# One head group of the first attention reordered: query copies behind the maxima, one product in another bank, transposes behind a product, one weight split behind a scaling

## The reference, cut to what matters

```python
qkv = h @ w_in
q = rmsnorm_2(q.reshape(B, S, 16, 64), q_gain); k = rmsnorm_2(k...); 
scores = einsum(q, kb) * scale + bias            # each block of 128 rows sees itself and the block before
m = maximum(max(scores), sink); p = exp(scores - m)
probs = p / (sum(p) + exp(sink - m))
o = einsum(probs, vb);  return o @ w_out
```

## Time and profile before

| | |
|---|---|
| median of 3 runs | 2672.14 us (2670.05 to 2672.7) |
| the profiled execution | 2672.14 us, its span 2670.8 us |
| TensorE busy | 2642.5 us of the span |
| mean granted TensorE clock | 0.997 of full |
| the first attention | from about 1205 us to about 1360 us of the span |

### The profile page before, as it was taken

The page is one execution under the profiler, slowest core; times in us unless marked ns, Lnnn a source line. Parts: engine busy times, 40 slices in busy tenths (PEclk is TensorE's granted clock), DMA queues, the critical chain, the costliest instruction groups (busy, mean ns, idle before and its releaser), DMA issues.

```text
span 2670.8 us, 31302 instructions
## 1 busy us (share of the span) xinstructions
PE 2642.5 (99%) x12784; PEld 2216.1 (83%) x12784; DVE 1435.9 (54%) x2254; ACT 982.7 (37%) x1622; POOL 319.5 (12%) x388
## 2 busy tenths in 40 slices
PE   9999999999999999999999999999999999999999
PEld 8898888888887788779988888888888888888887
DVE  7637447565767444356874343453434676543433
ACT  4343334342454222236642222422223586422221
POOL 0000010000021000015530000100000586200000
PEclk9999999999999999999999999999999999999999
DMA  5322225523223444464323322233232101232321
GB/s 161 125 82 82 98 89 167 176 79 110 77 97 95 107 103 95 99 109 108 108 95 108 97 96 87 87 110 95 95 97 86 56 17 48 90 100 95 103 94 56
DMA packets 280936, 258.94 MB, mean 97 GB/s; under 512 B 40261, under 2 KB 275800, under 8 KB 280792
## 3 DMA queue, kind: packets, MB, share of 16 engines
q1 hardware_dynamic: 280775, 256.93, 32.4%
q10 hardware_dynamic: 16, 0.00, 0.0%
HBM read 242.23 MB, written 14.68 MB: 96 GB/s over the span
## 4 chain that ended last, share of the span: by engine, by line
PE 91%; DVE 4%; ACT 3%; issue 2%; POOL 1%; POOLq 0%; DVEq 0%; ACTq 0%
PE bank L1163 29%; PE bank L1165 29%; PE bank L1164 29%; PE bank L1321 1%; DVE Wl L1886 1%; POOL Wl L2446 0%; PE bank L1374 0%; PE bank L1174 0%; ACT Wh L1522 0%; PE bank L1470 0%; DVE Pl L2401 0%; POOL TMP L2453 0%; DVE Z L2393 0%; PE bank L1262 0%; DVE Hl L2358 0%
## 5 line engine op out<-in xcount | busy, mean ns | idle before, releaser
L1163 PE MATMUL bank<-Hh,Wl 128*128 128x512 f32 x2136 | 838.3, 392 | 1.8 <-DVE Hl L1905 1.8
L1165 PE MATMUL bank<-Hh,Wh 128*128 128x512 f32 x2136 | 832.1, 390 | 0.0
L1164 PE MATMUL bank<-Hl,Wh 128*128 128x512 f32 x2136 | 831.9, 389 | 0.0
L1886 DVE TENSOR_TENSOR Wl<-RAW,Wh 128x1024 fp32r<-128x1024 f32 (+2 forms) x420 | 493.7, 1219 | 161.9 <-ACT Wh L1522 161.1
L1522 ACT ACTIVATE Wh<-RAW 128x1024 fp32r<-128x1024 f32 (+2 forms) x454 | 441.1, 1022 | 363.1 <-PE bank L1165 337.3
L1163 PEld LDWEIGHTS bank<-Hh,Wl 128*128 128x128 f32 x2136 | 401.4, 188 | 88.1 <-DVE Hl L1905 3.1
L1163 PE MATMUL bank<-Ph,Wl 128*128 128x512 f32 x1200 | 470.9, 392 | 0.8 <-DVE Wl L1886 0.4
L1165 PEld LDWEIGHTS bank<-Hh,Wh 128*128 128x128 f32 x2136 | 401.4, 188 | 84.1
L1164 PEld LDWEIGHTS bank<-Hl,Wh 128*128 128x128 f32 x2136 | 401.6, 188 | 83.9 <-issue 1.7
L1165 PE MATMUL bank<-Ph,Wh 128*128 128x512 f32 x1200 | 467.3, 389 | 0.0
L1164 PE MATMUL bank<-Pl,Wh 128*128 128x512 f32 x1200 | 466.8, 389 | 0.0
(11 more groups left out here) (336 smaller groups left out, 2424.7 us busy)
## 6 DMA issues: line engine op xcount, KB each, us to landing
RAW<-in_ffn_wg SPq DMA_DIRECT2D x44, 1024.0 KB, 5.4
RAW<-in_ffn_wu SPq DMA_DIRECT2D x44, 1024.0 KB, 5.3
RAW<-in_ffn_wd SPq DMA_DIRECT2D x32, 1024.0 KB, 5.1
RAW<-in_w_up SPq DMA_DIRECT2D x22, 1024.0 KB, 5.1
RAW<-in_w_in SPq DMA_DIRECT2D x20, 1024.0 KB, 5.1
RAW<-in_ffn_wd SPq DMA_DIRECT2D x16, 768.0 KB, 4.4
bias_scratch<-M SPq DMA_DIRECT2D x16, 512.0 KB, 8.1
RAW<-in_w_down SPq DMA_DIRECT2D x8, 1024.0 KB, 5.2
```

Of the source, the lines that this page charges most:

```text
L1163: mm(o, ll, rh, start=start, stop=False)
L1164: mm(o, lh, rl, start=False, stop=False)
L1165: return mm(o, lh, rh, start=False, stop=stop)
L1886: tt(Wl[:, n % 3, x:y], RAW[:, n % 2, x:y], f(Wh[:, n % 3, x:y]), ALU.subtract).then_inc(*w_lo.up(*([("w_lo", n)] if i else [])))
```

## The change

In the first attention's loop four things move:

1. `q_out` of one unit per head now stands behind `a_scores(i)` and `a_soft(i)` instead of ahead of them. Unit 6 comes at i = 0, where it had come at i = 1.
2. `q_product(8)` (i = 1) takes its bank from `banks` instead of the single slot of `products`.
3. `q_turn(g)` at i = 2 and i = 6 comes behind `q_product(7 + i)` instead of ahead of it. At i = 10 there is no product to stand behind.
4. Tile 110 (the last group's query weights) is split, and tile 112 loaded, behind `a_exp(1)` and `a_norm(1)` instead of at the head of `q_product(8)`.

```diff
     def q_product(u, ring=None):
         g, b = u // 4, u % 4
         if b == 0:
-            tile[g] = next_tile("aq", g, 1)
+            tile[g] = next_tile("aq", g, 0 if g == 2 else 1)
         (ring or (products[0] if products else banks)).take(("aq", g, b))
...
     for i in range(16 + LV):
-        for u in {0: (5,), 1: (6, 7)}.get(i, (6 + i,) if i < 10 else ()):
-            q_out(u)
+        if i == 0:
+            q_out(5)
         if i == 10:
             banks.join(products[0])
         if i < 16:
             for m in range(2):
                 scored.take(("a_s", i, m))
             do("a_scores", i)
             do("a_soft", i)
+            if i < 10:
+                q_out(6 + i)
             if i == 1:
                 do("a_k_low", 1)
             if i + 2 < 16:
                 do("a_bias", i + 2)
         if 0 <= i - LT < 16:
             turns(i - LT)
         if i in (1, 5, 9):
             do("a_q_norm", i // 4 + 1)
+        if i < 9:
+            q_product(7 + i, banks if i == 1 else None)
         if i % 4 == 2 and i < 11:
             q_turn(i // 4 + 1)
-        if i < 9:
-            q_product(7 + i)
         if i >= LV:
             values(i - LV)
         if i < 16:
             do("a_exp", i)
             do("a_norm", i)
+        if i == 1:
+            split()
+            load()
```

More of the change, by code:

```diff
@@ L653, in order @@
     now["low"] = "pool"
-    attend_a_order(steps, banks, tmps, next_tile, norm_step, hkeys, pv, xv, h_new, h_pair, stats, add_x, do, dense)
+    attend_a_order(steps, banks, tmps, next_tile, split, load, norm_step, hkeys, pv, xv, h_new, h_pair, stats, add_x, do, dense)
     now["low"] = "dve"
@@ L697, in out_partial, with attend_a_order @@
     return run
-def attend_a_order(steps, banks, tmps, next_tile, norm_step, hkeys, pv, xv, h_new, h_pair, stats, add_x, do, dense):
+def attend_a_order(steps, banks, tmps, next_tile, split, load, norm_step, hkeys, pv, xv, h_new, h_pair, stats, add_x, do, dense):
     do("a_begin")
```

## The result

The changed kernel takes 2685.08 us (median of 4 runs, 2684.63 to 2686.61) against 2671.52 us of the kernel before beside it (4 runs): a ratio of 1.0052, 95% interval 1.004 to 1.0065. It is slower by 13.6 us. The forecast was 2684.7 us. The profiled execution took 2684.63 us, its span 2683.4 against 2670.8 us. TensorE's busy time hardly moved (2644.2 against 2642.5 us).

What follows compares the result with a forecast made beforehand. TensorE, busy for all but about 1%, was taken as the bound, so only its waits or clock count. 2672.1 + 8.2 (orders: 3.8 + 2.9 + 1.5) + 4.4 (clock) = 2684.7 us; range 2674 to 2691.

Steps and rivals of the forecast that it cites:

- The bound: Whole kernel: TensorE is busy for all but about 1%, so only its waits or a slower clock move the time.
- The three long ones: TensorE's idle ahead of products 8, 10 and 14: 3.9, about 4.1 and about 3.2 us.
- Parts 1 and 2: Product 8 waits for `a_k_low(1)` to vacate its bank, product 10 for ScalarE's chain behind the later `q_turn(1)`: 3.8 us together.
- Part 3: Tile 110's split behind `a_norm(1)`: removes head 1's 1.7 us wait, a gain already inside the 3.8 us; costs nothing.
- Part 4: `q_turn(2)` behind `q_product(13)`: transposes start one product later, ScalarE's chain is the same, so product 14 starts 2.9 us later.
- one sign: First attention: no more TensorE wait for L2500, the line of the head 1 scaling wait.
- Part 5: i = 9 and 10: unit 15's later sum and the shifted `banks` rotation start output unit 7 1.5 us later.
- `("a_qt", 3, 0)` now gets the slot of output unit 4: i = 10: the slot, no longer slot 5, is vacated by an addition, so `q_turn(3)` starts at 1302.3 instead of 1301.46.
- The clock: Behind the three long waits: two falls to half the granted clock at 2.2 us each, 4.4 us.
- Rival (a): The orders cost 8.2 us and the clock keeps its full level: 2680.3 us; chance 0.17.
- The orders' 8.2 us: First attention: cost of the new order without the clock, 3.8 + 2.9 + 1.5 = 8.2 us.

Runs made afterwards that it cites:

- run 6: The changed kernel with 28 unread transposes of the identity ahead of product 8 and 28 ahead of product 10: 2680.09 us, ratio 1.0032 to the kernel before.
- Run 3: The changed kernel with the low parts of the second head's keys made at i = 0 instead of i = 1: 2680.70 us, ratio 1.0031 to the kernel before.
- run 1: The changed kernel with the group's transposes ahead of the product again (i = 2 and 6): 2675.69 us, ratio 1.0015 to the kernel before.
- run 4: The changed kernel with the copies of units 9 and 13 ahead of the exponentials of heads 2 and 6 on ScalarE: 2676.94 us, ratio 1.0017.
- Run 5: The changed kernel with transposes ahead of the product again and product 8 in the products' own slot: 2672.71 us, ratio 1.0005 to the kernel before.
- run 9: The changed kernel with units 11 and 15 copied and summed ahead of the maxima again, rotation still shifted: 2684.25 us, ratio 1.0043.
- run 7: The changed kernel with the rotation of the banks ring set back by one at i = 7: 2686.79 us, ratio 1.0058 to the kernel before.
- run 8: The kernel before with the split behind head 1's scaling, unit 6's copy at i = 0, units 9 and 13 copied ahead of the exponentials: 2670.07 us.
- run 2: The changed kernel with product 8 back in the products' own slot: 2681.14 us, ratio 1.0032 to the kernel before.
- run 10: The kernel of run 8 with unit 11's copy also moved ahead of the attended heads' pair at i = 4: 2671.07 us, ratio 0.9996.

## Why the prediction was right

**The bound.** TensorE's waits and clock decided, as said. In the stage 11.4 us of waits replace 3.6. The three long ones were forecast as 3.9, 4.1 and 3.2 us and came as 3.6, 3.8 and 2.65 (in two pieces).

**Parts 1 and 2, up to product 10: 3.8 us expected, 3.6 measured** (product 10 in run 6, without the clock's share: 22.61 against 19.02). Product 8's start was off by 0.1 us. Run 3 shows its cause alone, runs 1 and 4 that of product 10's wait. That `banks` had no free slot was readable in the code: the next slot's holder was still to be worked on.

**Part 3, the split: nothing.** The wait for head 1's scaling went and was worth nothing, because product 10 behind it wasn't ready: the scaling ended at 1247.55 us (forecast 1247.8), and product 10 started at 1258.79. Run 5, where ScalarE's chain is back in its old place, points to what it is worth with that: 0.7 us at product 10, from transposes that started no earlier than before. No run puts the split alone back, so this is read from the timelines and not shown by an experiment.

**Part 4: 2.9 expected, 2.76 measured** (10.17 - 7.41). A wait of 0.68 us for the scaled head 5 and 1.97 for ScalarE share it. So one sign failed: a wait for the line that was L2500 was still there, because the later sum of unit 11 also delays that scaling. It cost nothing of its own: in run 9, with this sum ahead of the maxima, it is gone, product 14 waits 2.87 us for ScalarE alone, and from product 11 to product 14 it takes 21.96 us, 21.94 with the change.

**Part 5: 1.5 expected, 1.5 measured, but by one cause and not two.** The prediction put it on the later sum and on the shifted rotation. Run 9 removes it with the rotation shifted, run 7 keeps it with the rotation set back. The step "`("a_qt", 3, 0)` now gets the slot of output unit 4" was true and cost nothing of its own: it split one wait into two.

**The clock: 4.4 expected, 5.3 measured.** The number and the size were both off, in opposite ways: three falls and not two, of 1.75 us on average and not 2.2. They cost 2.56 us behind product 8, 7.25 - 6.02 = 1.23 from product 10 to 11, and 8.63 - 7.16 = 1.47 from product 14 to the scores of head 8, each time the change against run 6's profile. Rival (a), full clock throughout, falls with the rows at 0.50; what the clock costs is shown by run 6. By the Trainium skill's page "TensorE: Matmul & The Clock Gate" (the table under "Why this matters for your kernels") idle gaps between bursts of matmuls put the clock back to half. The traces agree: 13.6 us at half level in the stage.

**The sum.** 3.6 + 2.8 + 1.5 + 5.3 = 13.2, of which 0.2 were won back up to head 15: 12.9 us of stage. The orders' 8.2 us were over by 0.5 (3.6 + 2.8 + 1.5 - 0.2 = 7.7) and the clock's 4.4 under by 0.9. The forecast difference was 12.6 us, the medians differ by 13.6; it started from 2672.1 us where 2671.52 was measured beside the change, which hides 0.6 of that. So a part of the nearness of 2684.7 to 2685.08 us is luck. The clock could have moved it by more: in run 9's profile nearly the same waits bring the scores of head 8 at 60.44 us from the first scores instead of 62.99, 2.6 us less by the clock alone.

## What to carry to other kernels

Where each queue is served in order, a step that is moved back on the bound engine delays everything behind it on the engine that serves it: add up that queue up to the instruction which vacates the bound engine's next buffer, and compare with the work that lies between. A buffer is free when the last reader of its last holder is done, not when the ring has a slot to give; look up that holder and its place in the reader's queue. On this TensorE, 99% busy, a removed wait was worth little (1.9 us won at product 10 in run 8 left 0.5 us of stage), while new waits of 3.6 and 3.8 us cost their length and the clock besides.

## What the runs showed of the hardware

- All ten waits of TensorE between 3.3 and 3.8 us brought half the granted clock (in the change, runs 1 to 4, 7 and 9): it fell between 1.7 us before the end of the wait (run 4) and 1.5 us after it (run 7, product 10, with TensorE busy again). Of the five places where 0.7 and 2.0 us of idle stand around 1 us of transposes, four did (the change, runs 2, 3 and 7) and one didn't (6); run 9's single wait of 2.9 us didn't either. In the stage, waits up to 1.7 us standing alone never did.
- The same wait doesn't bring the same stretch: with product 8's 3.62 us the clock was at half for 3.4 us (runs 1, 7, 9) or 6.8 us (the change, run 4). From product 8 to the next scores it took 4.2 to 4.5 us in the former and 5.2 to 5.3 in the latter, so this alone moves a run by about 1 us.
- In the second attention, which no kernel here changes, the clock was at half for 10.2 us in the kernel before, 3.4 us in the changed one and not at all in run 1. The time of one kernel goes with its mean clock: beside runs 1 to 10 the kernel before took 2670.0 to 2671.2 us in 31 executions, all at 0.998 or 0.999, and 2672.0 to 2674.1 us in 31 others, 29 of them at 0.997. In which stage these lost it was not recorded.
- 56 transposes that nobody reads, 3.2 us of them in each of two waits, gave back 3.8 us up to product 11, in the one execution that was profiled.
